# Splitting 128-token stationary blocks into two of 64 in a value projection and a prompt attention (hybrid decoder step)

## What is computed (the reference, cut)

```python
proj = h @ w_in                                   # h: tokens x 1024
z, xbc, dt_raw, q, k, v = split_in(proj)          # v: 2 heads x 64; dt_raw: 8
...
p = sink_probs(s, sinks).astype(v.dtype)          # prompt: 8 query heads, blocks of 128
o = (jnp.einsum('bnqkgd,bjkd->...', p_meta, v_meta)
     + jnp.einsum('bnkgqj,bnjkd->bnqkgd', p_band, v_band))
```

## Time and profile before

| What | Value |
|---|---|
| Time, median of three runs | 1594.99 us |
| Time of the profiled execution | 1598.22 us |
| Its span, first to last instruction | 1596.5 us |
| PE busy | 1548.9 us, 97% |
| PE's weight loads busy | 1305.1 us, 82% |
| VectorE, ScalarE, GpSimd busy | 284.1, 204.8, 131.4 us |
| Mean granted TensorE clock | 0.984 of full |

### The profile page before, as it was taken

How to read it: one execution, slowest core, us unless ns; L and a number is a source line. 1 busy time by engine, 2 the same in 40 slices (tenths; PEclk the granted TensorE clock), 3 DMA queues, 4 the chain that set the end, 5 groups by cost and what they waited for, 6 DMA issues and landing times.

```text
span 1596.5 us, 44448 instructions
## 1 busy us (share of the span) xinstructions
PE 1548.9 (97%) x20574; PEld 1305.1 (82%) x20574; DVE 284.1 (18%) x680; ACT 204.8 (13%) x527; POOL 131.4 (8%) x200
## 2 busy tenths in 40 slices
PE   7999999999999999998999999999999999999998
PEld 5667666666666667666999999999999999999897
DVE  2455520000000245553100000000000000000021
ACT  1245310000000034521000000000000000000000
POOL 4311125000000020111100000000000000000100
PEclk9999999999999999999899999999999999999999
DMA  9933429976323432332899999999999999999991
GB/s 250 269 114 89 128 82 273 334 246 218 119 93 113 112 112 67 100 117 93 280 355 343 358 359 352 357 346 339 369 349 355 356 346 359 344 365 360 348 354 36
DMA packets 199228, 397.39 MB, mean 249 GB/s; under 512 B 13723, under 2 KB 69667, under 8 KB 198889
## 3 DMA queue, kind: packets, MB, share of 16 engines
q1 hardware_dynamic: 180664, 346.26, 63.4%
q0 software_dynamic: 16816, 45.42, 9.4%
q10 hardware_dynamic: 1568, 2.91, 0.6%
HBM read 359.87 MB, written 36.63 MB: 248 GB/s over the span
## 4 chain that ended last, share of the span: by engine, by line
PE 95%; DVE 2%; issue 1%; ACT 1%; DMA 1%; SPq 0%; DVEq 0%; ACTq 0%
PE bank L1298 33%; PE bank L1320 16%; PE bank L1210 13%; PE bank L755 7%; PE bank L1227 6%; PE bank L1051 2%; PE bank L738 2%; PE bank L1068 2%; PE bank L724 1%; PE bank L1035 1%; PE bank L1024 1%; PE bank L1260 1%; PE bank L678 1%; PE bank L709 1%; PE bank L1041 1%
## 5 line engine op out<-in xcount | busy, mean ns | idle before, releaser
L1298 PE MATMUL bank<-arena,ring 128*64 128x108 f32 x11264 | 532.9, 257 | 9.6 <-issue 8.7
L1298 PEld LDWEIGHTS bank<-arena,ring 128*64 128x64 f32 x11264 | 526.8, 138 | 15.5 <-issue 13.1
L1320 PE MATMUL bank<-arena,ring 128*64 128x108 f32 x5632 | 263.2, 256 | 0.2
L1320 PEld LDWEIGHTS bank<-arena,ring 128*64 128x64 f32 x5632 | 261.7, 137 | 0.8 <-issue 0.6
L1210 PE MATMUL bank<-hnT,ring 128*128 128x336 f32 x704 | 200.8, 449 | 1.8 <-DVE hnT L1676 1.8
L1210 PEld LDWEIGHTS bank<-hnT,ring 128*128 128x128 f32 x704 | 134.6, 191 | 68.1 <-issue 3.2
L755 PE MATMUL bank<-hnT,ring 128*128 128x336 f32 x384 | 119.8, 457 | 0.0
L2133 DVE TENSOR_TENSOR arena<-arena,bank 128x432 f32<-128x432 f32 (+1 forms) x48 | 27.2, 567 | 509.3 <-PE bank L1298 509.3
L1227 PE MATMUL bank<-arena,ring 128*128 128x336 f32 x352 | 99.6, 446 | 0.0
L755 PEld LDWEIGHTS bank<-hnT,ring 128*128 128x128 f32 x384 | 70.5, 192 | 34.7 <-issue 6.4
L1227 PEld LDWEIGHTS bank<-arena,ring 128*128 128x128 f32 x352 | 66.9, 190 | 32.6
(11 more groups left out here) (360 smaller groups left out, 1079.1 us busy)
## 6 DMA issues: line engine op xcount, KB each, us to landing
ring<-in_moe_w_gate SPq DMA_DIRECT2D x88, 1024.0 KB, 6.2
ring<-in_moe_w_up SPq DMA_DIRECT2D x88, 1024.0 KB, 6.3
ring<-in_moe_w_down SPq DMA_DIRECT2D x88, 1024.0 KB, 5.9
ring<-in_w_in SPq DMA_DIRECT2D x16, 1024.0 KB, 6.7
ring<-in_w_gate SPq DMA_DIRECT2D x11, 1024.0 KB, 20.6
ring<-in_w_up SPq DMA_DIRECT2D x11, 1024.0 KB, 18.5
xg_rows<-arena POOLq DMA_DIRECT2D x1, 10800.0 KB, 71.8
y_rows<-arena POOLq DMA_DIRECT2D x1, 10800.0 KB, 112.8
```

Source lines behind the costliest of these rows:

```text
L1298: ins = mm(into[rows, SLOTS * fi:SLOTS * fi + SLOTS], weights[:, c, col:col + 64], xg[:, k0 + c, :], start=(k0 + c == 0 and fi == 0), stop ...
L1320: ins = mm(bank[5 + c // 4][rows, SLOTS * (c % 4):SLOTS * (c % 4) + SLOTS], weights[:, col:col + 64], hid[:, f, :], start=(f == 0 and c % ...
```

## The change

Every stationary block of 128 tokens in the two places becomes two of 64, whose outputs go to partitions 0 to 63 and 64 to 127 of the same bank. In the third tile of the value projection, with 80 tokens, the two blocks have 64 and 16 tokens, for `min(r0 + 64, n)` ends the second at 80. The number of matmuls doubles there: 96 passes a layer for the value projection, and 12 a head for the attention. The moving operands, the sums and the semaphores stay as they are.

```diff
                     for k in range(DK):
                         if i == 0:
                             pe.wait_ge(hn_ready, 8 * 2 * l + k + 1)
-                        ins = mm(bank[1][0:n, 136 * i:136 * i + 136], hnT[:, k, t0:t0 + n], vdt[:, k, :], start=(k == 0), stop=(k == DK - 1))
+                        for r0 in (0, 64):
+                            r1 = min(r0 + 64, n)
+                            ins = mm(bank[1][r0:r1, 136 * i:136 * i + 136], hnT[:, k, t0 + r0:t0 + r1], vdt[:, k, :], start=(k == 0), stop=(k == DK - 1))
                 ins.then_inc(proj_psum, 1)
...
                     wait_probT(hd)
-                    mm(bank[7][:, cols], PT[:, 0:128], vtok[:, 0, h], start=True, stop=True)
-                    mm(bank[0][:, cols], PT[:, 128:256], vtok[:, 0, h], start=True, stop=False)
-                    mm(bank[0][:, cols], PT[:, 256:384], vtok[:, 1, h], start=False, stop=True).then_inc(att_psum, 1)
+                    for out, q0, keys, first, done in ((bank[7], 0, 0, True, True), (bank[0], 128, 0, True, False), (bank[0], 256, 1, False, True)):
+                        for r0 in (0, 64):
+                            ins = mm(out[r0:r0 + 64, cols], PT[:, q0 + r0:q0 + r0 + 64], vtok[:, keys, h], start=first, stop=done)
+                    ins.then_inc(att_psum, 1)
```

## The result

The changed kernel takes 1603.45 us (median of 6 runs, 1601.89 to 1608.39) against 1593.05 us in the runs beside it: a ratio of 1.0067, 95% interval 1.0048 to 1.0086. The medians are 10.4 us apart, and the interval is 7.6 to 13.7 us. The profiled execution took 1602.75 us with a span of 1601.0.

The account below looks back on a forecast made before the run. PE's order of work was taken to bound the kernel. Value projection 8.0, attention 0.6 and clock 2.0 sum to +10.6 us on the 1595.0 median, so 1605.6 us, range 1595.5 to 1611.

Parts of the forecast that it names:

- The bound: Whole kernel: PE's order of work is the critical path; gains or losses in the changed places reach the end nearly one-for-one.
- Tiles 0 and 1: Value projection: tile 1's pairs cost 0.116 us like whole passes, so nothing; tile 0 hides its change, about -0.05 us.
- Tile 2: Value projection's third tile: 64 and 16 columns alternate with a width change per block; layer pays +4.0 us, two layers +8.0.
- L709's exposed load: Line after the value projection: its first load is exposed behind tile 2's narrow blocks, +0.10 us.
- the way out: Return from 64-column halves to full width: 0.20 us before 336 moving columns, 0.16 before transposes.
- L778's gap: 0.38 us before the 8-column L778 where 0.283 is normal, taken as a sign that few columns use another layout.
- Attention: Per head 0.66 us against 0.62, so +0.04; 14 heads remain, +0.6 us in all.
- The clock: Granted clock falls to 0.50 behind tile 2: 1.5 falls at 1.3 us, +2.0 us; bounds 0 and +3.9.
- The number: Whole kernel: +10.6 us on the median of 1595.0, so 1605.6 us, 0.7% slower.

Follow-up runs that it names:

- the pair of 32 and 33 columns: Changed kernel with the third tile's second block padded to 32 or 33 columns, against the kernel before: 1.0030 with 32, 0.9995 with 33.
- the doubled one: Changed kernel with the third tile's 64 and 16 token blocks computed twice over: 1.0132 against the kernel before, 21 us over it.
- the padded kernel: Changed kernel with the third tile's second block widened to 64 columns by other tokens or zeros: 0.9989 against the kernel before.
- the grouped order: Changed kernel with the third tile's eight blocks of 64 first, then its eight of 16: 1.0035 against the kernel before.

## Why the prediction was right, and where it was off

- **The bound.** PE's order of work set the end. What the value projection lost reached the end: doubling the third tile added the 5.69 us of its row in layer 0, and for the 19.5 us expected in all the runs gave 21, with an interval of 15 to 27.
- **Tiles 0 and 1: nothing.** Right. 0.1 us a layer when they are halved alone, and the ratio is 0.9987.
- **Tile 2: +4.0 us a layer.** Right in mechanism and size: 3.84 us. Two small errors partly cancel in it. I had 0.365 for a block and read 0.34 (16 columns) and 0.37 (64 columns), so 5.7 us and not 5.84; and I put L709's exposed load at 0.10 where the earlier trace rows already gave 0.20 for the way out, and it cost 0.20 (4.72 against 4.52). That 16 columns take another layout than 64 was a guess from L778's gap; the changed kernel's steps show it, and the pair of 32 and 33 columns shows where the border lies. The rule of the Trainium skill that was weighed there (TensorEngine Tiling (Array Packing), "Key Properties": a change of mode drains, a change of tile doesn't) agrees with these runs: 0.71 us for one k with 64 and 16 columns, 0.23 with equal layouts, and 7.96 against 4.16 us for the stretch with 32 and with 33 columns.
- **Attention: +0.04 a head.** Right, 0.02 to 0.03; the run with the attention alone gave 0.9994. The same skill says (TensorE: Matmul & The Clock Gate, "The mechanism", in Part 3) that a weight load overlaps with matmuls in flight only when its row group differs, though a few lines above it also lets a load into a background buffer go ahead. The two halves have the same 128 rows, and yet the padded third tile keeps 0.116 us a pair. Whole blocks overlap too: if loading and streaming took turns, their 0.103 us with 64 moving columns would be 0.103 + 0.283 x 72/336 = 0.164 with 136, and it is 0.116. Here the measurement decides against the "only": no row group has to differ, and these runs don't show that the column group has to.
- **The clock: +2.0 us.** This step failed. I took the fall behind L778 to L788 as a likeness of what tile 2 would become. In none of ten such stretches, in five traces (the changed kernel twice, the third tile alone, the 32 columns, the doubled one), did the clock fall within the third tile or right behind it, not even when the stretch was 11.3 us long. What falls there are lie in the first two tiles' stretch, where the kernel before has one as well (532.1 us). The term is zero; the sum by the trace is 2 x 3.84 + 14 x 0.03 = 8.1 us.
- **The number.** 1605.6 us was forecast and 1603.45 measured, +10.6 against +10.4. This agreement owes something to luck. 8.1 us lies within both intervals of the change (7.6 to 13.7 and 4.3 to 9.6), 10.6 only within the first. The profiled pair alone would have misled in the other direction, 1601.0 - 1596.5 = 4.5 us. Falls of the clock are a part of that, and they differ both ways. The execution before had two, at 532 and 580 us, that the one after has not, and they cost 1.25 us (its L724 took 8.72 us in layer 1, 7.47 in layer 0) and 1.4 us (3.75 against 2.36). The one after had two, at 158 and 196 us (granted clock 0.50 and 0.51), that the one before has not. And ahead of the experts the one before ran at 0.50 from 750.6 to 771 us, the one after only from 759 to 769: from layer 1's L709 to the first expert matmul it took 767.5 - 538.4 = 229.1 us before and 773.5 - 548.6 = 224.9 after, although 0.4 us more was due.
- **Why single executions differ so much.** From the first expert matmul to the end all kernels run the same code. It took 1596.5 - 767.5 = 829.0 us before, 1601.0 - 773.5 = 827.5 after, 822.2 in the padded kernel (from 767.6 to 1589.8), 820.6 in the doubled one (786.8 to 1607.4) and 831.6 with the third tile alone split (770.2 to 1601.8); all thirteen traces lie between the last two. A spread of 11 us, larger than the effect, lies where nothing was changed. PE's idle time before the expert matmuls, put down to "issue" in the view by source, goes along with it: 9.4 us in the doubled kernel, 12.2 in the padded one, 21.8 before (the view of waits in the earlier trace rows has 8.7 of these), 25.9 with the third tile alone split. What makes these gaps I have not settled.

## What to carry to other kernels

Look at the remainder before you cut a tile. Halves of 64 columns stream side by side for the price of a whole and save load time where few columns move, but a remainder of 32 columns or fewer takes another layout, and alternating the two pays the drain at every step; pad it to 33 or more, or leave that tile whole. To finish one width before the other is only half a cure: it saved 1.74 of 3.84 us here. Where wide and narrow blocks must alternate, put as many narrow ones together as the order allows: a change of width cost about 0.15 us in and 0.15 to 0.2 us out, just over the 0.27 us that six halved passes of 64 moving columns earn. And when an effect is under 1%, add it up from the stages of the trace: here it gave 8.1 us, while two sets of runs gave 10.4 and 7.7 between the medians.

## What the runs showed of the hardware

- One column of width decides: a block of 32 stationary columns beside one of 64 costs 3.8 us in sixteen pairs of passes, a block of 33 nothing (7.96 and 4.16 us for the stretch, the second as with 64).
- A block's columns don't count for the streaming: with 16, 80 or 128 stationary columns a pass of 136 moving ones takes the same 0.116 us when nothing is drained (the grouped order's 16-wide passes, whose starts lie that far apart from 29.33 to 30.95 us, and the earlier trace rows). So does a pair of 64 and 64 or of 64 and 33 side by side.
- A stretch of 11.3 us in which the weight loads were busy for 4.80 us kept the full clock of 2.4 GHz (granted clock 1.00). The lines L778 to L788 were followed by half of it, 1.2 GHz, in layer 1 of the kernel before, and in layer 0 they were not the earlier trace rows. In other executions it is the other way round: with the attention alone halved a fall begins at 69.8 us, behind the same lines in layer 0.
